# Two of four heads' probabilities normalised on ScalarE instead of GpSimd in the wide turns of a two-layer trunk's sparse attention

## What is computed

```python
def block(args):
    ...
    score = jnp.where(key_pos[None, None, :] <= t[None, :, None], score, -jnp.inf)
    _, idx = lax.top_k(score, n_sel)
    ...
    s = jnp.einsum('bthgd,btkhd->bhgtk', q_blk, k_sel).astype(jnp.float32) * (HEAD_DIM ** -0.5)
    s = jnp.where(sel_ok[:, None, None], s, -jnp.inf)
    pr = jax.nn.softmax(s, axis=-1)
    return jnp.einsum('bhgtk,btkhd->bthgd', pr.astype(v_sel.dtype), v_sel)
```

## Time and profile before

| | |
|---|---|
| median of 3 runs | 1166.92 us (1164.58 to 1167.45) |
| the profiled execution | 1166.92 us, its span 1165.1 us |
| granted TensorE clock, mean over the span | 0.985 of full |
| TensorE busy | 1116.0 us, 96% of the span |
| VectorE, ScalarE, GpSimd busy | 600.7, 450.2, 192.3 us |
| GpSimd's normalisation (L541) | 128 instructions, 84.4 us, mean 690 ns |
| waits of that group for the reciprocal (L1100) | 89.7 us |

### The profile page before, as it was taken

The page is one execution under the profiler, slowest core; times in us unless marked ns, Lnnn a source line. Parts: engine busy times, 40 slices in busy tenths (PEclk is TensorE's granted clock), DMA queues, the critical chain, the costliest instruction groups (busy, mean ns, idle before and its releaser), DMA issues. The chain is left out here.

```text
span 1165.1 us, 15098 instructions
## 1 busy us (share of the span) xinstructions
PE 1116.0 (96%) x5577; PEld 896.5 (77%) x5577; DVE 600.7 (52%) x1106; ACT 450.2 (39%) x854; POOL 192.3 (17%) x338
## 2 busy tenths in 40 slices
PE   7999999999999999999899787999999999999997
PEld 6776678988888888888667665658988888888885
DVE  4353544543543643647377976634553453553554
ACT  6376554241321321335354366553332322322322
POOL 1354520000000000005303268340000000000004
PEclk9999899999999999999999889999999999999999
DMA  7431403354444344442423314003353543443431
GB/s 220 91 73 37 109 1 73 73 126 94 90 107 98 84 107 100 84 106 56 113 42 73 72 37 109 1 1 73 73 125 75 109 108 74 107 108 76 105 73 72
DMA packets 50782, 97.71 MB, mean 84 GB/s; under 512 B 4448, under 2 KB 4640, under 8 KB 50720
## 3 DMA queue, kind: packets, MB, share of 16 engines
q1 hardware_dynamic: 50208, 96.78, 36.5%
q10 hardware_dynamic: 512, 0.11, 0.1%
HBM read 94.78 MB, written 2.10 MB: 83 GB/s over the span
## 5 line engine op out<-in xcount | busy, mean ns | idle before, releaser
L1789 PE MATMUL bank<-w_hi,r_hi 128*128 128x512 f32 x512 | 199.3, 389 | 0.0
L1791 PE MATMUL bank<-w_hi,r_lo 128*128 128x512 f32 x512 | 199.2, 389 | 0.0
L1790 PE MATMUL bank<-w_lo,r_hi 128*128 128x512 f32 x512 | 199.2, 389 | 0.0
L1013 DVE SCALAR_TENSOR_TENSOR w_lo<-w_raw,gT,w_hi 128x512 fp32r<-128x512 f32 x152 | 104.5, 751 | 149.3 <-ACT w_hi L678 149.2
L1468 PE MATMUL bank<-r_hi,w_hi 128*128 128x512 f32 (+1 forms) x456 | 177.5, 389 | 0.0
L1469 PE MATMUL bank<-r_hi,w_lo 128*128 128x512 f32 (+1 forms) x456 | 177.4, 389 | 0.0
L1470 PE MATMUL bank<-r_lo,w_hi 128*128 128x512 f32 (+1 forms) x456 | 177.4, 389 | 0.0
L678 ACT ACTIVATE w_hi<-w_raw,gT 128x512 fp32r<-128x512 f32 x152 | 97.1, 713 | 174.7 <-PE bank L1791 103.7
L1003 DVE TENSOR_TENSOR w_lo<-w_raw,w_hi 128x2048 fp32r<-128x2048 f32 x34 | 78.3, 2302 | 124.7 <-ACT w_hi L670 124.7
L670 ACT ACTIVATE w_hi<-w_raw 128x2048 fp32r<-128x2048 f32 x36 | 68.9, 1913 | 157.5 <-PE bank L1791 118.7
L1790 PEld LDWEIGHTS bank<-w_lo,r_hi 128*128 128x128 f32 x512 | 96.1, 188 | 20.1
(11 more groups left out here) (169 smaller groups left out, 1664.7 us busy)
## 6 DMA issues: line engine op xcount, KB each, us to landing
w_raw<-in_w_mlp_up SPq DMA_DIRECT2D x64, 512.0 KB, 6.0
w_raw<-in_w_mlp_down SPq DMA_DIRECT2D x64, 512.0 KB, 6.4
w_raw<-in_b_w_in SPq DMA_DIRECT2D x16, 512.0 KB, 6.3
w_raw<-in_a_w_in SPq DMA_DIRECT2D x8, 512.0 KB, 6.7
w_raw<-in_a_w_out SPq DMA_DIRECT2D x8, 512.0 KB, 5.6
w_raw<-in_b_w_out SPq DMA_DIRECT2D x8, 512.0 KB, 5.9
X<-in_x SPq DMA_DIRECT2D x4, 512.0 KB, 6.7
w_raw<-in_a_w_in SPq DMA_DIRECT2D x8, 256.0 KB, 7.2
```

The source lines that it names most:

```text
L1013: last = nc.vector.scalar_tensor_tensor(out=w_l[:, cs], in0=w_raw[:, slot, cs], scalar=g, in1=w_h[:, cs].bitcast(f32), op0=ALU.mult, op1=A ...
L1789: nc.tensor.matmul(bank[:], xh, hi[:, k, :], start=h == 0 and k == 0, stop=False)
L1790: nc.tensor.matmul(bank[:], xh, lo[:, k, :], start=False, stop=False)
L1791: ins = nc.tensor.matmul(bank[:], xl, hi[:, k, :], start=False, stop=h == 1 and k == 3)
```

## The change

In turns of layer 1 with over two key blocks (turns 8 to 15) GpSimd normalises heads 0 and 1 of the four, and ScalarE heads 2 and 3, with an activation that copies and scales by the same reciprocal. ScalarE's two instructions stand at the end of step n for turn n+1, behind the square sums and ahead of the next step's `o_high` and `pt_copy`. TensorE waits for a second semaphore before the first transpose of such a turn. The other turns are as before.

```diff
--- before.py
+++ after.py
@@ -62,6 +62,19 @@
 for _l in range(DEPTH):
     for _n in range(TURNS):
         PT_AT.append(PT_AT[-1] + len(key_blocks(_l, turn(_l, _n)[1])))
+
+
+def shared(layer, n):
+
+    return len(key_blocks(layer, turn(layer, n)[1])) > 2
+
+
+
+P_NO, P_ACT_NO = [0], [0]
+for _l in range(DEPTH):
+    for _n in range(TURNS):
+        P_NO.append(P_NO[-1] + (2 if shared(_l, _n) else 4))
+        P_ACT_NO.append(P_ACT_NO[-1] + (2 if shared(_l, _n) else 0))
 
 
 def pt_of(layer, n):
@@ -256,7 +269,7 @@
         ki_t, ki_hi_done, ki_lo_done, wi_done = sem("ki_t"), sem("ki_hi_done"), sem("ki_lo_done"), sem("wi_done")
         idx_ready, idx_relu, idx_acc, top_v = sem("idx_ready"), sem("idx_relu"), sem("idx_acc"), sem("top_v")
         s_ready, s_masked, sink_put, exp_done = sem("s_ready"), sem("s_masked"), sem("sink_put"), sem("exp_done")
-        inv_done, p_done = sem("inv_done"), sem("p_done")
+        inv_done, p_done, p_act_done = sem("inv_done"), sem("p_done"), sem("p_act_done")
         pt_ready, pt_out, pv_done = sem("pt_ready"), sem("pt_out"), sem("pv_done")
         o_hi_done, o_lo_done = sem("o_hi_done"), sem("o_lo_done")
         sq_done, yg_done, yg_last_done, ms_done, rs_y_done, x_new = (sem("sq_done"), sem("yg_done"), sem("yg_last_done"), sem("ms_done"),
@@ -536,7 +549,7 @@
                 N = 16 * layer + n
                 W = width(layer, turn(layer, n)[1])
                 pool.wait_ge(inv_done, N + 1)
-                for c in range(4):
+                for c in range(2 if shared(layer, n) else 4):
                     v = probs[:, N % 3, c, 0:W]
                     nc.gpsimd.tensor_tensor(v, v, inv_sum[:, N % 3, c:c + 1].to_broadcast([P, W]), ALU.mult).then_inc(p_done, 1)
 
@@ -771,6 +784,14 @@
                 nc.scalar.activation(v, v, ACT.Exp, bias=neg_max[:, N % 3, c:c + 1], scale=-1.0,
                                      accum_out=row_sum[:, N % 3, c:c + 1]).then_inc(exp_done, 1)
 
+            def normed(layer, n):
+
+                N = 16 * layer + n
+                act.wait_ge(inv_done, N + 1)
+                for c in range(2, 4):
+                    v = probs[:, N % 3, c, 0:width(layer, turn(layer, n)[1])]
+                    nc.scalar.activation(v, v, ACT.Copy, scale=inv_sum[:, N % 3, c:c + 1]).then_inc(p_act_done, 1)
+
             def pt_copy(layer, K):
                 act.wait_ge(pt_ready, K + 1)
                 if K >= PT_PLACES:
@@ -819,6 +840,8 @@
                             j, c, h = (s - FILL_OUT[layer]) // 4, (s - FILL_OUT[layer]) % 4 // 2, s % 2
                             if h:
                                 y_square(norm, j, c)
+                    if n + 1 < TURNS and shared(layer, n + 1):
+                        normed(layer, n + 1)
                     for u in SPLITS[layer].get(n, ()) if n >= 0 else ():
                         split(u)
                 o_high(layer, 7)
@@ -1647,7 +1670,9 @@
                 K = PT_AT[N] + c
                 bank = t_free(layer, ("pt", K))
                 if c == 0:
-                    pe.wait_ge(p_done, 4 * N + 4)
+                    pe.wait_ge(p_done, P_NO[N + 1])
+                    if shared(layer, n):
+                        pe.wait_ge(p_act_done, P_ACT_NO[N + 1])
                 for e in range(4):
                     ins = nc.tensor.transpose(bank[:, blk(e)], probs[:, N % 3, e, blk(c)], ident[:, 0:P])
                 ins.then_inc(pt_ready, 1)
```

## The result

The change makes the kernel slower by a little. Over 16 runs each, the median goes from 1166.74 us to 1169.05 us (1167.9 to 1171.32). The ratio of the comparison is 1.0026, with a 95% interval of 1.0018 to 1.0033: 2.1 to 3.9 us. The forecast was 1170.0 us, 0.27% over before. The interval lies above 1, so the loss is real, and its centre is under the bound of 0.3%.

A forecast was written before the change was run, and what follows sets the result against it. TensorE, working in nearly the whole span, was taken to bound the kernel. Turn 9's 0.0, turn 15's 1.6 and the clock's 1.5 summed to 3.1 us over 1166.9, giving 1170.0 us; range 1167.0 to 1172.2.

The forecast's parts named there:

- The removed work is worth 0: Turns 8 to 15: taking two heads off GpSimd gains 0, since TensorE never waits for it there; 1.6 us spare at tightest.
- The copy's price and the queue: ScalarE's added copies: 0.53 us each at 384 columns, 0.61 at 512, holding up what stands behind them in its in-order queue.
- Turn 9: 0.0: Step 8: VectorE's low half 0.33 us late less 0.28 returned, rounded 0.0 us; bounds -0.2 and 0.4.
- the returned 0.28 us of VectorE: Turn 9: VectorE's small sum takes 0.19 us instead of 0.47 because GpSimd is done earlier.
- That rival: Turn 9: a longer idle gap brings a second loss of clock, another 1.5 us, 1171.5 us in all; chance 0.15.
- the rival's own test: Second loss of clock at turn 9: decided by whether the clock is still low at 732 us.
- Turns 10 to 14: 0: Steps 9 to 13: the copies' delays are covered by TensorE's other work or by slack, so they cost 0.
- the thinnest cover: Turn 13, step 12: masks ready at 761.3, wanted by TensorE at 761.73; slack 0.4 us, the least expected.
- the sign that I had named: The forecast would be wrong if TensorE waited elsewhere in turns 8 to 15, above all before step 13's scores (761.73).
- Turn 15: 1.6: Step 14: the output's high half shifts, delaying TensorE's turning of x by 1.6 us; bounds 1.3 and 1.8.
- The clock: 1.5, likelier than not: After turn 15's wait grows from 0.8 to 2.4 us, TensorE's clock falls, costing 1.5 us; bounds 0 and 1.7.
- the count of cases (five in six): In the earlier profile, five of six TensorE waits above 1.8 us behind the start-up were followed by a clock fall.

The follow-up runs named there:

- The kernel with the copies behind: Against the change: ScalarE's same sixteen scaled copies placed behind its copies of the transposed probabilities; 1165.92 us, ratio to before 0.9999.
- the single turn: Against the change: only turn 15 shared between ScalarE and GpSimd, turns 8 to 14 all GpSimd's; 1168.79 us, ratio to before 1.0028.
- the filled kernel: Against the change: eight unread matmuls added on TensorE in its wait before the turning of x in step 15; 1168.63 us, ratio to before 1.0023.
- one head: Against the change: in turns 8 to 15 ScalarE normalises one head and GpSimd three; 1167.03 us, ratio to before 1.0008.
- the two reordered kernels: Against before: masks and transposed copies first in odd steps 9 to 15, extra top-k round in step 9 (1163.37 us, 0.9975) or 6 (1162.08 us, 0.9959).

## Why the prediction was right

**The removed work is worth 0.** Right. TensorE never waited for GpSimd in turns 8 to 15, and the two waits elsewhere are unchanged. The kernel with the copies behind relieves GpSimd in the same way without the harm, and gains nothing that can be measured.

**The copy's price and the queue.** Right. Two copies hold the queue 1.03 us at 384 columns (721.21 to 722.24) and 1.24 at 512 (774.43 to 775.67), by pairs against 1.06 and 1.22 in the sum.

**Turn 9: 0.0.** Right up to the scores (0.07), and the returned 0.28 us of VectorE came as worked out. As a term it was too small: distance A grew by 0.60. The step that failed is the sentence that priced the clock at turn 15 only and left turn 9 to a rival. That rival gave the mechanism, a low stretch twice as long, and this came: 0.28 x 12 = 3.4 us of full clock lost instead of 0.14 x 12 = 1.7. But by the rival's own test, a clock that is still low at 732, it did not come. The low stretch ends 8.1 us behind turn 9's reciprocal, and 7.9 us behind it in the kernel before; it grew at its front.

```profile
722.00:723.00 1.00, 0.00 (x0) 0.64 0.00 0
723.00:729.00 6.00, 5.26 (x22) 0.50 0.00 0
729.00:730.00 1.00, 1.00 (x10) 0.94 0.00 0
```

These windows of TensorE with the change put it at 722.3 to 729.1. Its first 2.6 us lie ahead of the scores of 724.86, where TensorE idles or runs a weighted sum and then still waits 0.39 us for the masks. So the rival's price was wrong too, 1.5 us where 0.6 was measured.

**Turns 10 to 14: 0.** Right in size. But the thinnest cover was turn 10's and not turn 13's: the turning of x in step 10 waits 0.17 us. By the sign that I had named (TensorE waiting elsewhere in turns 8 to 15) that is a small miss.

**Turn 15: 1.6.** Measured 1.58, in the change and the single turn alike, and 1.57 in the filled kernel.

**The clock: 1.5, likelier than not.** It fell in all three profiles in which this wait was 2.37 us, for 1.60 to 1.63. The profiles with a wait of 1.76 and of 2.97 had no fall, so the length of a gap alone does not decide, and the count of cases (five in six) was a fair guide to the chance and no more.

The sum in the profile is 0.6 + 1.58 + 1.63 = 3.8 us for turns 9 and 15, the forecast 3.1, the measured ratio 3.0. That the forecast and the timed value lie 0.1 us apart is partly luck: turn 9's 0.6 us is missing from the forecast, and the timed runs give less than the profile, though 3.8 is inside their interval of 2.1 to 3.9. The span of the profiled execution is only 1.5 us over that of before; turn 8's reciprocal came 2.4 us earlier in it (713.19 against 715.62), in code that the change does not touch. One profile against one profile would have given the wrong size.

## What to carry to other kernels

Before moving work to an idle engine, look at what stands behind it in that engine's queue, and not at its load: the same sixteen copies cost 3 us ahead of a copy that TensorE waits for, and nothing behind it. Work taken off an engine is worth only what someone waited for it, and here eight turns had 1.6 us and more to spare. And where a wait before dense matmuls grows as here, from 0.8 to 2.4 us, count the clock as well: it cost as much again as the growth of the wait (1.6 us each).

## What was not expected

- The loss can nearly all be bought back without removing a wait: twenty idle matmuls in two gaps took the ratio from 1.0026 to 1.0003.
- A gap of 2.97 us left the clock at its full level, while gaps of 2.37 us were followed by a fall in three profiles of three. Gaps of 2.04 and 2.57 in the kernel before had gone the same two ways. Even the same gap goes either way. The one of 2.57 us (2.57 or 2.58 in every profile) stands in code that no edit touches; the clock behind it held in four of the twelve profiles (among them the kernel before) and fell in eight (among them the change), where it was 0.51 to 0.54 over the next 3 us.
- An operation on one number per row (the mean square) takes 0.47 or 0.48 us on VectorE in turn 9 where GpSimd still multiplies (before, only turn 15, one head), and 0.21 in the seven profiles of shared turns in which GpSimd is done by then. But GpSimd being busy is not enough: in the two reordered kernels, with GpSimd in the middle of its four heads, the same sum takes 0.22 and 0.21 us in turn 9 and 0.81 in turn 14. In these two profiles and in the three with 0.47 or 0.48 it ends within 0.15 us after a head's multiply ends, so its length looks like what was left of that multiply. That is read off seven rows and not tested.
